# A 30-column pad removed and a one-word tensor moved, so that the on-chip memory addresses shift

## The reference, cut to what matters

```python
D_MODEL, SEQ, MEM_LEN = 1024, 512, 256
# first block
x = x + hybrid_mixer(rmsnorm(x))            # differential and forgetting attention, gates, w_o
x = x + memory_cross_attention(rmsnorm(x), rmsnorm(mem))
x = x + (relu(rmsnorm(x) @ w1) ** 2) @ w2   # 1024 -> 4096 -> 1024
x = rmsnorm(x, g_final)
# second block, two layers
for l in (0, 1):
    x = x + (pool_conv_mixer if l == 0 else mla_attention)(rmsnorm(x))
    x = x + memory_cross_attention(rmsnorm(x), rmsnorm(mem_2))
    x = x + (silu(conv3(h @ w_up_g)) * (h @ w_up_a)) @ w_down   # h = rmsnorm(x); 1024 -> 2816 -> 1024
return rmsnorm(x)
```

## Time and profile before

| | |
|---|---|
| median of 3 runs | 2654.39 us (2649.92 to 2655.05) |
| the profiled execution | 2649.92 us, span of its instructions 2647.0 us |
| mean granted TensorE clock | 0.961 |
| PE busy, PEld busy | 2448.9 us (93%), 1927.8 us (73%) |
| DVE, ACT, POOL busy | 1291.7 us, 963.5 us, 1010.1 us |
| chain that ended last | PE 80%, DVE 11%, ACT 4%, issue 4%, POOL 1% |
| DMA | 215.52 MB, mean 81 GB/s |

### The profile page before, as it was taken

One profiled execution on the slowest core, in us unless ns is written; L12 is line 12 of the kernel. 1 busy time (PEld: TensorE's weight loads), 2 busy tenths in 40 slices (PEclk: granted clock), 3 DMA queues, 4 the chain that ended last, 5 costly groups with the idle time before them and its releaser, 6 DMA issues.

```text
span 2647.0 us, 29999 instructions
## 1 busy us (share of the span) xinstructions
PE 2448.9 (93%) x11166; PEld 1927.8 (73%) x11166; DVE 1291.7 (49%) x2129; ACT 963.5 (36%) x1408; POOL 1010.1 (38%) x736
## 2 busy tenths in 40 slices
PE   5997999899999999865899999997889999999998
PEld 4783747796888888654777888885555886888887
DVE  3115282523333335897335655554666424555555
ACT  3136244333422223521543322225556533322223
POOL 2440403522444444452333555544330332544443
PEclk8997989999999999887999999999999999999999
DMA  4320203241222222230212222222100340323221
GB/s 125 96 81 16 64 1 111 80 144 64 99 97 95 95 95 96 80 96 32 87 41 97 96 96 95 95 96 64 46 17 2 127 143 32 100 99 101 99 95 64
DMA packets 175466, 215.52 MB, mean 81 GB/s; under 512 B 6432, under 2 KB 157522, under 8 KB 175350
## 3 DMA queue, kind: packets, MB, share of 16 engines
q1 hardware_dynamic: 175350, 213.97, 24.7%
HBM read 211.84 MB, written 2.11 MB: 81 GB/s over the span
## 4 chain that ended last, share of the span: by engine, by line
PE 80%; DVE 11%; ACT 4%; issue 4%; POOL 1%; DMA 0%; DVEq 0%; SPq 0%; ACTq 0%; POOLq 0%
PE ps_l L706 70%; DVE arena L2113 3%; PE ps_l L911 2%; PE ps_l L1020 2%; PE ps_l L824 1%; PE ps_s L957 1%; ACT w_hi L1181 1%; POOL w_lo L558 1%; PE ps_s L1003 1%; DVE a_lo L1676 1%; DVE arena L1670 1%; DVE arena L2136 1%; DVE x_T L1955 0%; DVE arena L1806 0%; DVE x_T L2088 0%
## 5 line engine op out<-in xcount | busy, mean ns | idle before, releaser
L558 POOL TENSOR_TENSOR w_lo<-w_raw,w_hi 128x512 fp32r<-128x512 f32 x732 | 1009.9, 1412 | 1610.7 <-ACT w_hi L1181 1610.7
L706 PE MATMUL ps_l<-a_hi,w_hi 128*128 128x512 f32 (+1 forms) x1984 | 789.2, 398 | 89.4 <-POOL w_lo L558 31.4
L706 PE MATMUL ps_l<-a_lo,w_hi 128*128 128x512 f32 (+1 forms) x1984 | 781.1, 394 | 0.0
L706 PE MATMUL ps_l<-a_hi,w_lo 128*128 128x512 f32 (+1 forms) x1984 | 780.2, 393 | 0.0
L1181 ACT ACTIVATE w_hi<-w_raw 128x2048 fp32r<-128x2048 f32 x197 | 375.8, 1908 | 661.1 <-PE ps_l L706 636.7
L706 PEld LDWEIGHTS ps_l<-a_hi,w_hi 128*128 128x128 f32 (+1 forms) x1984 | 374.2, 189 | 183.7 <-issue 48.2
L706 PEld LDWEIGHTS ps_l<-a_lo,w_hi 128*128 128x128 f32 (+1 forms) x1984 | 374.0, 189 | 86.0 <-issue 4.8
L706 PEld LDWEIGHTS ps_l<-a_hi,w_lo 128*128 128x128 f32 (+1 forms) x1984 | 373.7, 188 | 83.9 <-issue 1.2
L706 PE MATMUL ps_l<-b_hi,w_hi 128*128 128x512 f32 (+1 forms) x896 | 330.8, 369 | 11.3 <-DVE b_lo L1973 9.6
L706 PE MATMUL ps_l<-b_lo,w_hi 128*128 128x512 f32 (+1 forms) x896 | 329.5, 368 | 0.0
L706 PE MATMUL ps_l<-b_hi,w_lo 128*128 128x512 f32 (+1 forms) x896 | 329.5, 368 | 0.0
(11 more groups left out here) (254 smaller groups left out, 2578.0 us busy)
## 6 DMA issues: line engine op xcount, KB each, us to landing
w_raw<-in_ffn_w_up_dram SPq DMA_DIRECT2D x44, 1024.0 KB, 5.0
w_raw<-in_w_dram SPq DMA_DIRECT2D x32, 1024.0 KB, 5.2
w_raw<-in_ffn_w_down_dram SPq DMA_DIRECT2D x22, 1024.0 KB, 4.9
w_raw<-in_w_in_dram SPq DMA_DIRECT2D x20, 1024.0 KB, 5.3
w_raw<-in_xa_wkv_dram SPq DMA_DIRECT2D x16, 1024.0 KB, 5.5
w_raw<-in_w_kv_mem_dram SPq DMA_DIRECT2D x8, 1024.0 KB, 5.5
w_raw<-in_xa_wq_dram SPq DMA_DIRECT2D x8, 1024.0 KB, 5.1
w_raw<-in_xa_wo_dram SPq DMA_DIRECT2D x8, 1024.0 KB, 5.1
```

Of the source, the lines that this page charges most:

```text
L558: e.tensor_tensor(w_lo[:, b % 2, o], w_raw[:, b % 2, o], w_hi[:, b % 2, o].bitcast(F32), ALU.subtract).then_inc(w_lo_made[by], 1)
L706: ins = pe.matmul(o, *((v, w) if swap else (w, v)), start=first and n == 0, stop=last and n == 2)
```

## The change

`keep` loses its 30 unused columns, so that its rows are 776 bytes long and no longer 896. `forget_bias`, one number in 8 partitions, is allocated between `small` and `ck8` and no longer at the very end. With the rounding to 32 bytes this gives the following places (bytes in a partition).

| tensors | start before, modulo 256 | start after, modulo 256 | shift |
|---|---|---|---|
| `x_T`, `a_hi`, `a_lo`, `b_hi`, `b_lo`, `w_raw`, `w_hi`, `w_lo`, `keep` | 128 | 128 | 0 |
| `cols`, `rst`, `ident_bf`, `mask_bf`, `ones`, `small` | 0 | 160 | -96 |
| `ck8` | 0 | 192 | -64 |
| `wf_raw`, `wf_hi`, `wf_lo`, `arena`, `a2_hi`, `a2_lo`, `cum` | 128 | 64 | -64 |

No instruction is added, removed or moved on any engine, and no semaphore wait changes. One line less stands ahead of L450, so that line numbers behind it are lower by one in the changed file.

```diff
-        keep = sb("keep", [P, P + 96])[:, 0:P + 66]
+        keep = sb("keep", [P, P + 66])
         ident = keep[:, 0:P]
...
-        g08 = small[:, 9:10]
+        bf_col, g08 = sb("forget_bias", [8, 1])[:, :], small[:, 9:10]
...
         cum = sb("cum", [8, T])[:, :]
-        bf_col = sb("forget_bias", [8, 1])[:, :]
...
-            sp.dma_start(keep, keep_d).then_inc(ld_keep, 16)
+            sp.dma_start(keep[:, :], keep_d).then_inc(ld_keep, 16)
```

## The result

The changed kernel takes 2678.05 us (median of 4 runs, 2676.03 to 2679.36), the kernel before 2653.90 us (4 runs, 2649.92 to 2655.05). The ratio is 1.0096, with a 95% interval of 1.0083 to 1.0108: slower by 24 us. The forecast, 2654 us and no change, was wrong, and the time lies outside its range of 2645 to 2670 us. It is 1 us from what rival 1 gave at its upper bound (2677), the part of rival 1 that the range left out. The experiments show that the agreement is luck: the price of rival 1 fits, and its mechanism is wrong.

A forecast was written before the change was run, and what follows sets the result against it. The prediction took PE's pace on L706 to bound the kernel. Every term was valued 0: 2649.9 + 0 = 2649.9 us for the profiled execution, 2654.4 us for the median, stated as 2654, range 2645 to 2670 us.

The forecast's parts named there:

- rival 1: PE streams a2 more slowly, at most 6.7 ns on each of 3456 matmuls, 23 us, 2677 from the median; chance 0.22.
- upper bound: On a2 products in L706: a partly used 64-byte head streams like 16 columns more, 6.7 ns, 3456 matmuls, 23 us.
- What bounds the kernel: PE busy 93% of the span; L706 fills the three feed-forward windows, so each nanosecond on its matmuls comes out whole.
- `a2_hi` and `a2_lo`, from 128 to 64 modulo 256: The 3456 L706 matmuls streaming from this pair: cost between 0 and 23 us, value taken 0.
- the row on the weight loads: Loads of `wf_hi` slices starting 0, 32, 64, 96 bytes past multiples of 128: 87, 88, 88 ns least, median, most.
- The other float32 matmuls: About 1500 matmuls on the arena and `ones`, the largest group transposes: at most 10 us, value taken 0.
- ACT, DVE, GpSimd: Durations not changed by start places: ACT below 0.1 us, DVE bound 0.2 us, GpSimd tiles unmoved; value 0.
- DMA: Moved landing places of x and memory rows, and moved output stores: within 0.2 us either way, value 0.
- Rival 2: DVE's collisions with GpSimd fall otherwise: half of L2113's waits gone, 9 us faster, 2645, or slower by as much; chance 0.10.
- Its 1.1 us: In Rival 2, the extra time of the slow level of DVE taps, said to be what one GpSimd subtraction takes.

The follow-up runs named there:

- e3: The kernel before with 64 unused bytes ahead of `x_T`, so every tensor starts 64 bytes further on: 2652.92 us against 2651.89.
- e5: The kernel before with `w_hi` and `w_lo` alone 64 bytes further on, later tensors kept in place modulo 256: 2697.84 us against 2653.90.

## Why the prediction was wrong, point by point

- **What bounds the kernel** was right. L706 is the bound; each nanosecond of it came out at the end (23.6 us by the trace, 24 between the medians).
- **The step that failed** is "*`a2_hi` and `a2_lo`, from 128 to 64 modulo 256*", in its "Value taken: 0, by the row on the weight loads". It measured +6.6 ns on each of 3456 matmuls. The row was a wrong witness, for it times the load, and what pays is the stream beside it. The witness needed was the next line, 389/397/397, or the pace on `dq2`.
- **The upper bound** of that step, 6.7 ns and 23 us, came from 16 columns x 0.417 ns and fits the measured 6.6 ns by luck: its reason, a head of 64 bytes, is refuted: with all tensors moved by 64 (e3) no matmul is slower, and 32 to 224 bytes, 64 aside, cost alike.
- **The assumption under it** was never argued: that a cost of place would depend on one operand's start. PE reads two operands at once, the streamed one and the next weights (in the first feed-forward window PEld is busy for 269.90 of 326.00 us beside it), and the table of the change shows that a2 moves against `w_hi` and `w_lo`.
- The Trainium skill, "SBUF — State Buffer", section "Who interferes with whom", gives PE two independent read ports, one for each of these, and says that PE never waits on anyone. That is said of one engine against another, and no run here contradicts it. But the two reads of PE itself are not independent in the runs: 700 ns a product against 680, by the distance of the two alone. Whether the memory or PE causes it, they don't say.
- **The other float32 matmuls**: right. In most of them both operands lie in the arena, so that their distance stays. In the transposes of L823, which was L824, it does change, for one operand is the identity in `keep`; they have 90.0 us busy and had 88.9, but e3, where no distance changes, has 90.2, and at full clock they most often follow each other at 109 ns in all three. No effect is seen on these.
- **ACT, DVE, GpSimd**: right, by the rows above. **DMA**: the medians of the earlier trace rows are as before, but for x at the head, 6.8 us for 6.5, which is 0.3 and not at most 0.2 us and could as well be the scatter of two DMAs. Rival 2 did not happen. (Its 1.1 us was read loosely: the least of the earlier trace rows is 1257 ns.)
- **The chances**: 0.24 for slower was too little. The prediction found no full-size case of the new place of the streamed operand, and let "not seen" weigh as "no effect"; the full-size case of the distance, `dq2`, it didn't look for.

## What to carry to other kernels

Where TensorE's pace is the bound, look at the start addresses of what streams and of the weights that are loaded beside it, modulo 256 bytes, and keep their distance under control: a length changed anywhere ahead of them can move them apart by 32 bytes and cost 3% of each matmul like these, 128 x 128 weights and 512 columns. When a change moves addresses, compare pairs of operands that one engine reads together, not single operands. And when a row serves as the witness for a cost, read the duration of every instruction that runs beside it, not just the one that names the tile.

## What the runs showed of the hardware that was not expected

- Matmuls with weights of 128 x 128 and 512 streamed columns, rounded float32, at a granted clock of 1.00 take 226.7 ns if streamed operand and weights are a multiple of 256 bytes apart, and 229 to 234 ns at the seven other multiples of 32.
- Moving all operands together by 64 or 128 bytes changes nothing (2652.92 and 2652.62 us against 2651.89).
- With 256 columns a distance of 0 is the slow one: 120 ns against 114 to 118 on average at 64 and 192.
- At the lower clock, with 427 ns a matmul, the distance costs nothing (e5).
- Open: the cause of the dent at 64, why 64 weight columns take 230 ns at a distance of 0, how the cost is split over a product, and what the fixed 13 ns of a matmul consist of.
